# A mixture-of-experts stage on one core: the first token tile is turned and split in two halves, the second tile's transposes go inside the first product, and part of the next weights waits for the first gather

## What is computed

```
gate = jnp.sum(jax.nn.one_hot(ids, N_EXPERTS, dtype=jnp.float32) * wv[..., None], axis=1)
hid = jnp.einsum('td,edf->tef', t, w_up)
a, u = jnp.split(hid, 2, axis=-1)
act = jax.nn.silu(a) * u * gate.astype(hn.dtype)[..., None]
y = jnp.einsum('tef,efd->td', act, w_down)
```

## Time and profile before

| | |
|---|---|
| median of 3 runs | 883.4 us (883.09 to 884.41) |
| the profiled execution | 883.04 us |
| its span in the trace | 881.0 us, 2.04 us less than its time |
| PE busy, PEld, DVE, ACT, POOL | 90%, 71%, 68%, 40%, 35% of the span |
| the expert stage | from about 544 us to the end |

### The profile page before, as it was taken

How to read it: one execution, slowest core, us unless ns; L and a number is a source line. 1 busy time by engine, 2 the same in 40 slices (tenths; PEclk the granted TensorE clock), 3 DMA queues, 4 the chain that set the end, 5 groups by cost and what they waited for, 6 DMA issues and landing times. The chain is left out here.

```text
span 881.0 us, 13284 instructions
## 1 busy us (share of the span) xinstructions
PE 791.8 (90%) x4729; PEld 623.6 (71%) x4730; DVE 596.6 (68%) x701; ACT 354.3 (40%) x644; POOL 309.3 (35%) x248
## 2 busy tenths in 40 slices
PE   3899999999988899999999994199999999998593
PEld 3689999999945565667776883178888888887341
DVE  6779489742178965776786575994557997670097
ACT  3810111101345763454455343544444444443044
POOL 3000899940000101100000011155566888563046
PEclk9999999999968999999999995599999999999697
DMA  8956534530170501311102047867778997789664
GB/s 322 402 175 215 167 123 134 168 96 1 64 300 29 143 14 49 96 72 41 56 25 72 25 146 255 326 237 280 265 259 333 400 374 285 276 298 320 260 245 155
DMA packets 77361, 165.30 MB, mean 188 GB/s; under 512 B 7397, under 2 KB 32517, under 8 KB 75266
## 3 DMA queue, kind: packets, MB, share of 16 engines
q1 hardware_dynamic: 68402, 132.15, 42.7%
q0 software_dynamic: 7760, 28.31, 8.8%
q10 hardware_dynamic: 1152, 4.19, 1.3%
HBM read 132.57 MB, written 32.08 MB: 187 GB/s over the span
## 5 line engine op out<-in xcount | busy, mean ns | idle before, releaser
L2040 PE MATMUL psum<-we_hi,x_parts 128*128 x384 | 137.0, 403 | 0.8 <-ACT au L1897 0.8
L1703 DVE TENSOR_TENSOR we_lo<-we_raw,we_hi 128x2048 fp32r<-128x2048 f32 x48 | 116.5, 2433 | 1.4
L449 PE MATMUL psum<-hn_hi,w_hi 128*128 128x364 f32 (+1 forms) x384 | 91.3, 333 | 2.4 <-issue 2.4
L1701 DVE CAST we_hi<-we_raw 128x2048 fp32r<-128x2048 f32 x42 | 56.2, 1339 | 53.3 <-DMA we_raw<-in_w_up_dram 27.2
L449 PE MATMUL psum<-hn_lo,w_hi 128*128 128x364 f32 (+1 forms) x384 | 90.8, 332 | 0.0
L449 PE MATMUL psum<-hn_hi,w_lo 128*128 128x364 f32 (+1 forms) x384 | 90.5, 330 | 0.0
L1037 PE MATMUL psum<-wo_hi,mixin 128*128 128x512 f32 (+1 forms) x256 | 83.6, 398 | 0.0
L2040 PEld LDWEIGHTS psum<-we_hi,x_parts 128*128 128x128 f32 x384 | 72.3, 188 | 15.2 <-issue 1.0
L2040 PE MATMUL psum<-we_lo,x_parts 128*128 x192 | 75.3, 392 | 0.0
L630 DVE SCALAR_TENSOR_TENSOR proj<-wm,cT,proj 128x2048 f32<-128x2048 f32 x28 | 72.5, 2637 | 0.0
L449 PEld LDWEIGHTS psum<-hn_hi,w_hi 128*128 128x128 f32 x384 | 67.3, 190 | 6.3 <-issue 6.0
(11 more groups left out here) (315 smaller groups left out, 1584.6 us busy)
## 6 DMA issues: line engine op xcount, KB each, us to landing
we_raw<-in_w_up_dram SPq DMA_DIRECT2D x32, 1024.0 KB, 8.1
wm<-in_w_mod_dram SPq DMA_DIRECT2D x16, 1024.0 KB, 5.6
we_raw<-in_w_down_dram SPq DMA_DIRECT2D x16, 1024.0 KB, 6.1
w_raw<-in_w_in_dram SPq DMA_DIRECT2D x16, 512.0 KB, 6.3
we_raw<-ff_d SPq DMA_DIRECT2D x12, 512.0 KB, 6.4
proj<-in_x_prompt_dram SPq DMA_DIRECT2D x4, 1024.0 KB, 8.0
sc_room<-in_w_mod_dram SPq DMA_DIRECT2D x4, 1024.0 KB, 14.2
proj<-in_w_mod_dram SPq DMA_DIRECT2D x2, 2048.0 KB, 12.0
```

Of the source, the lines that this page charges most:

```text
L449: mm = pe.matmul(psum[:, 3 * slot + c, 0:n], w[:, slot, k, :], hn[:, k, t0:t0 + n], start=(k == 0 and w is w_hi and hn is hn_hi), stop=(k ...
L1701: dve.tensor_copy(we_hi[:, a:b], raw).then_inc(wh_ready, 1)
L1703: dve.tensor_tensor(we_lo[:, a:b], raw, we_hi[:, a:b].bitcast(F32), ALU.subtract).then_inc(ready, 1)
L2040: mm = pe.matmul(psum[:, 2, :], x[:, s, k, :], w[:, bass.ds(at + k * 2 * DE, 2 * DE)], start=(k == 0 and x is x_hi and w is we_hi), stop=( ...
```

## The change

Five things are changed together.

1. SP: within expert 1, the second half of `w_up` (and so also its `w_down`, and expert 2, which come behind it in SP's program) waits for `gathered[0]` 16, that is for the landing of the first gather. Expert 2 no longer waits for `x_turned`.
2. PE: tile 0 is turned and lowered in two halves of four transposes and one product (`turn_first`, `lower_first`), each half with its own semaphore count.
3. ACT: tile 0's high and low part are copied in two halves of 128 x 512 (`high_first`, `low_first`) in place of copies of 128 x 1024. `up` of tile 0 waits for the first half ahead of k = 0 and for the second half ahead of k = 4.
4. PE: tile 1's eight transposes stand no longer ahead of `up` of tile 0 but inside it, after k = 4, and its `lower_x` after k = 6 (before: after k = 2).
5. The counts that the others wait for are moved up by one, since tile 0 now counts twice. POOL's third gather waits, as before, for the whole turned tile 0.

```diff
--- before.py
+++ after.py
@@ -1548,6 +1548,8 @@
                     sp.wait_ge(down_ready, e - (NW - 1))
                     sp.wait_ge(up_done, last)
                 for half in range(2):
+                    if e == 1 and half == 1:
+                        sp.wait_ge(gathered[0], 16)
                     a, b = at + half * UP // 2, at + (half + 1) * UP // 2
                     sp.dma_start(we_raw[:, a:b].rearrange("p (k n) -> p k n", k=KC // 2),
                                  up[:, half * KC // 2:(half + 1) * KC // 2, :]).then_inc(up_loaded[s][half], 16)
@@ -1557,7 +1559,6 @@
 
             for e in range(FIRST):
                 load(e)
-            sp.wait_ge(x_turned, 1)
             for e in range(FIRST, NW):
                 load(e)
             sp.wait_ge(tables_ready, 1)
@@ -1813,10 +1814,10 @@
 
             fetch_first(0, None)
             fetch_first(1, None)
-            fetch_first(2, 1)
-            fetch_first(3, 2)
+            fetch_first(2, 2)
+            fetch_first(3, 3)
             gate_act(0, None)
-            fetch_first(4, 3)
+            fetch_first(4, 4)
             gate_act(1, 1)
             less = pool.value_load(ntile[0:1, 0:1], min_val=SLOT_TILES_MIN // 2 - 1, max_val=SLOT_TILES // 2 - 2)
             with pool.Fori(1, less + 1) as i:
@@ -1869,13 +1870,23 @@
                     act.wait_ge(loaded, 16)
                     act.activation(we_hi[:, a:b], we_raw[:, a:b], ACT.Copy).then_inc(first_hi, 1)
 
+            def high_first(half):
+                act.wait_ge(x_turned, 1 + half)
+                src = psum[:, half, :].rearrange("p (k c) -> p k c", c=P)
+                act.activation(x_hi[:, 0, 4 * half:4 * half + 4, :], src, ACT.Copy).then_inc(xh_copied, 1)
+
+            def low_first(half):
+                act.wait_ge(x_lowed, 1 + half)
+                src = psum[:, half, :].rearrange("p (k c) -> p k c", c=P)
+                act.activation(x_lo[:, 0, 4 * half:4 * half + 4, :], src, ACT.Copy).then_inc(x_ready, 1)
+
             def high_x(t, s):
-                act.wait_ge(x_turned, t + 1)
+                act.wait_ge(x_turned, t + 2)
                 src = psum[:, 0:2, :].rearrange("p b (k c) -> p (b k) c", c=P)
                 act.activation(x_hi[:, s, :, :], src, ACT.Copy).then_inc(xh_copied, 1)
 
             def low_x(t, s):
-                act.wait_ge(x_lowed, t + 1)
+                act.wait_ge(x_lowed, t + 2)
                 src = psum[:, 0:2, :].rearrange("p b (k c) -> p (b k) c", c=P)
                 act.activation(x_lo[:, s, :, :], src, ACT.Copy).then_inc(x_ready, 1)
 
@@ -1909,8 +1920,10 @@
 
                 act.activation(idst[:, s:s + 1], ids[:, bass.ds(t, 1)], ACT.Copy).then_inc(idst_ready, 1)
 
-            high_x(0, 0)
-            low_x(0, 0)
+            high_first(0)
+            high_first(1)
+            low_first(0)
+            low_first(1)
             high_x(1, 1)
             low_x(1, 1)
             swish(0, None)
@@ -2001,8 +2014,19 @@
                                    start=(k % 4 == 0), stop=(k % 4 == 3), is_transpose=True, skip_group_check=True)
                 mm.then_inc(x_turned, 1)
 
+            def turn_first(half):
+                for k in range(4 * half, 4 * half + 4):
+                    mm = pe.matmul(psum[:, half, (k % 4) * P:(k % 4 + 1) * P], xg[:, 0, k * P:(k + 1) * P], ident[:, :],
+                                   start=(k % 4 == 0), stop=(k % 4 == 3), is_transpose=True, skip_group_check=True)
+                mm.then_inc(x_turned, 1)
+
+            def lower_first(half):
+                pe.wait_ge(xh_copied, 1 + half)
+                pe.matmul(psum[:, half, :], minus[:, :], x_hi[:, 0, 4 * half:4 * half + 4, :].rearrange("p k c -> p (k c)"),
+                          start=False, stop=True, skip_group_check=True).then_inc(x_lowed, 1)
+
             def lower_x(t, s):
-                pe.wait_ge(xh_copied, t + 1)
+                pe.wait_ge(xh_copied, t + 2)
                 for half in range(2):
                     mm = pe.matmul(psum[:, half, :], minus[:, :], x_hi[:, s, 4 * half:4 * half + 4, :].rearrange("p k c -> p (k c)"),
                                    start=False, stop=True, skip_group_check=True)
@@ -2030,10 +2054,13 @@
 
             def up(t, s, place, copied, between):
                 e, at = place
-                pe.wait_ge(x_ready, t + 1)
+                if not (isinstance(t, int) and t == 0):
+                    pe.wait_ge(x_ready, t + 2)
                 if copied is not None:
                     pe.wait_ge(au_copied, copied)
                 for k in range(KC):
+                    if isinstance(t, int) and t == 0 and k % (KC // 2) == 0:
+                        pe.wait_ge(x_ready, 1 + k // (KC // 2))
                     if k % (KC // 2) == 0:
                         pe.wait_ge(up_ready, e * 2 + (1 + k // (KC // 2)))
                     for x, w in ((x_hi, we_hi), (x_hi, we_lo), (x_lo, we_hi)):
@@ -2057,7 +2084,9 @@
                 mm.then_inc(down_done, 1)
 
             def step0(k):
-                if k == 2:
+                if k == 4:
+                    turn_x(1, 1, 16, 2)
+                elif k == 6:
                     lower_x(1, 1)
 
             def step1(k):
@@ -2068,14 +2097,16 @@
                 elif k == 5:
                     lower_act(0)
 
-            turn_x(0, 0, 16, None)
-            lower_x(0, 0)
+            pe.wait_ge(gathered[0], 16)
+            turn_first(0)
+            turn_first(1)
+            lower_first(0)
+            lower_first(1)
             pe.wait_ge(oneh_ready, 2)
             by_slot(7, 2, 6)
-            turn_x(1, 1, 16, 1)
             first, second = places(1)
             up(0, 0, first, None, step0)
-            turn_x(2, 0, 32, 2)
+            turn_x(2, 0, 32, 3)
             up(1, 1, second, 1, step1)
             down(0, first, None)
             less = pe.value_load(ntile[0:1, 0:1], min_val=SLOT_TILES_MIN // 2 - 1, max_val=SLOT_TILES // 2 - 2)
@@ -2089,7 +2120,7 @@
                         lower_act(t - 1)
 
                 if gathers is not None:
-                    turn_x(t + 1, 1 - s, gathers, t + 1)
+                    turn_x(t + 1, 1 - s, gathers, t + 2)
                 before, this = places(t)
                 up(t, s, this, t, steps)
                 down(t - 1, before, t - 1)
@@ -2108,7 +2139,7 @@
             lower_act(less * 2 + 3)
             down(less * 2 + 3, places(less * 2 + 4)[0], less * 2 + 3)
             pe.wait_ge(rows2_in, 16)
-            pe.wait_ge(x_ready, less * 2 + 4)
+            pe.wait_ge(x_ready, less * 2 + 5)
             half_row(l2g_row, l2g, 0)
             half_row(l2g_row, l2g, 1).then_inc(tail_sums, 1)
```

## The result

| | before | after |
|---|---|---|
| median | 883.6 us (883.09 to 884.41) | 897.0 us (896.07 to 898.47, 4 runs) |
| profiled execution | 883.04 us | 896.44 us |
| PE busy | 791.8 us | 794.7 us |

The ratio is 1.0146, with a 95% interval of 1.0128 to 1.0165. The forecast was 891.4 us, with 894.5 as the upper end.

A forecast was written before the change was run, and what follows sets the result against it. PE bounds the kernel: its tile loop has no gap, so delay ahead counts in full. 5.3 + 0.9 + 1.6 + 0.2 = 8.0 us on 883.04 gives 891.0, plus 0.4 for the median: 891.4 us; range 888.5 to 894.5.

The forecast's parts named there:

- The gather: First gather, with later weights held back: takes 4.5 us, landing at 567.0 instead of 569.1, a gain of 2.1 us.
- The rival that it isn't faster: First gather's 6.56 us could be descriptor work on POOL; all 2.1 us later, 893.5 us; chance 0.10.
- The held transfers are those that ACT waits for: ACT's casts precede tile 0's copies in order; the last cast would end at 577.85, against 570.2 before.
- I take 8.4: landing at 575.9: Expert 1's `w_down`, issued near 567.5, takes 8.4 us to land; ends 574.2 and 576.6.
- no cost: Expert 2's loads land behind expert 1's, near 585, ahead of DVE's need, hidden behind PE's products.
- First product at +5.3: After ACT's release, copies, lowering and gate products: the first product starts at 582.0 against 576.68, +5.3 us.
- Inside the first product: Tile 1's eight transposes move into the first product, 0.88 us at full clock: +0.9 us.
- Between the first and the second product: ACT's table load loses its cover behind tile 1's low copy; PE issues at +3.4 instead of 1.8: +1.6 us.
- The rival of a drain: A drain behind ACT's table load, exposed between the first two products: 892.5 us; chance 0.02.
- The clock: PE's clock rises at 582.2, just after the first product has begun: +0.2 us, ends 0 and 1.5.
- the clock stays low longer: Whole first product at half speed, as PE's work comes in pieces with a long pause: about 897 us; chance 0.04.
- The tile loop has no gap: PE is busy for 190.00 of 190.00 us between 594 and 784 us, so any delay ahead moves all that follows.

The follow-up runs named there:

- experiment 7: Changed kernel, with expert 2's transfers and POOL's third gather issued only when expert 1's `w_down` has landed: 894.6 us, one run.
- experiment 9: Changed kernel, with expert 2's transfers and the second and third gathers issued only when expert 1's `w_down` has landed: 896.0 us, one run.
- experiment 5: Changed kernel with the hold kept, the two casts that wait for held transfers moved from ACT to DVE: 883.6 us, ratio 0.9986 to the original.
- experiment 4: Changed kernel plus a one-column sigmoid on ACT behind tile 0's low copies, making the table load early: 894.8 us, ratio 1.0122 to the original.
- experiment 1: Original kernel with only SP's wait moved (the hold alone), tile 0 turned whole, transposes as before: 893.2 us, ratio 1.0098.
- experiment 2: Changed kernel without the hold, SP's original order restored, halves and moved transposes kept: 884.5 us, ratio 1.0008 to the original.
- experiment 3: Changed kernel, with expert 2's three transfers issued only when expert 1's `w_down` has landed: 895.5 us, ratio 1.0136 to the original.

## Why the prediction was right in kind and short in size

- **The gather**: landing forecast 567.0, measured 567.02. The rival that it isn't faster is wrong (4.47 us against 6.56). The Trainium skill (DMA: Bandwidth & Descriptors, "Queues, rings and completion order") says that a DMA engine takes turns between the rows that have work. Experiments 7 and 9 agree in kind, in the other direction: gathers on POOL's queue slow the weights on SP's, by 1.0 and 2.2 us. In size the prediction's estimate from it, 1.3 us lost, falls short of the 2.1 that holding gave.
- **"The held transfers are those that ACT waits for"**: right, and shown by experiment 5.
- **"I take 8.4: landing at 575.9"**: this step failed. It measured 11.70, landing at 579.2, 3.3 us of the 5.4 by which the sum was short. The nearest row, 9.1 us, was of a pair beside the third gather, and the third gather (its "gather 2") is all the company that the prediction gave to `w_down`. The pair with that gather is 7.5 + 1.0 us by experiments 7 and 9, just the 8.4 forecast. What it left out measured the rest: 2.2 us for the tail of the second gather, which is still in flight when the held transfers start, and 1.0 for expert 2's transfers, which SP now issues right behind. Those it had put at "no cost", looking only at who waits for them and not at what they delay.
- **First product at +5.3**: the rest of that path measured as forecast, from the cast's end at 581.08 to the product at 585.13, 4.1 us against 4.15.
- **"Inside the first product" +0.9**: 0.88 for the eight transposes and some 0.5 us of low clock, against 0.2 in the clock's term.
- **"Between the first and the second product" +1.6**: measured 1.6. The table load lost its cover, and experiment 4 shows it. The rival of a drain is wrong. The Trainium skill (ScalarE: Activation LUTs, "What ACT_TABLE_LOAD costs") gives 1.28 us and a drain of 1.38 behind it. The load took 1.28, but the sigmoid started 0.02 us later.
- **"The clock" +0.2**: this step failed too, by 1.9 us. I looked for the clock only where PE starts up, and not where the new gap of 3.5 us lets it fall. The second product measured 1.6 us longer, the first 0.5. The two failed terms together, 3.3 and 1.9, are 5.2 of the 5.4 us. The rival "the clock stays low longer" named the right time, 897, by luck: it had the whole first product at half speed, 6 us, where 1 us of it ran so, and the rest of the 897 is the landing.
- **The tile loop has no gap**: right, 190.00 of 190.00.
- **Small slips in the sums**, none of which changes the outcome: 582.1 + 0.5 + 6.7 is 589.3 and not 589.5; 894.2 with half a us is 894.7 and not 894.5; and the low end is 888.5 in one place and 888.0 in another.

By parts timed alone: hold +8.7, halves -1.8, transposes and table load +2.5, together 9.4 of the 12.9 us that the ratio gives. The other 3.5 us are no more than the intervals leave open, since the hold's alone reaches 3 us either way. Counted within the traces, from the start of the stage to tile 3's transposes, hardly anything is left over: 49.2 us before, 62.3 after, 59.2 in experiment 1 and 52.2 in experiment 2. So the hold alone adds 10.0 us and the rest of the change 3.0, together 13.0 of 13.1. Each is one trace, and the clock takes its part in each of them: it falls in the changed kernel's gap (1.6 us), and it rises late in experiment 2.

Two things stay open. The clock fell in the gap of about 3.5 us, or within half a us behind it, in all four traces that have the long pause of ACT's wait ahead and nothing added in the gap (after, experiments 3, 7, 9: pauses of 12.5, 11.5, 10.5 and 8.3 us). It didn't in experiments 2 and 5, which have the same gap but no pause between tile 0's turning and its lowering. What decides isn't shown. And the second gather's tail costs `w_down` 2.2 us, while all of its 0.5 MB are 1.3 us at 414 GB/s; why was not tried.

## What to carry to other kernels

Before a transfer is held back, look up which engine's program waits for it, and what stands behind that wait. Here it was right to hold the transfer (2.5 us gained, with its casts moved), and wrong to leave its cast on ACT, ahead of the copies that set the pace. A wait also has a price where it ends: count what goes out in the same microsecond, and look at every gap that it makes in PE's work for the clock, since the same work behind it may run slower; work that must be done anyway and has no hurry (the gate products) is what such a gap is for.

## What was not expected of the hardware

- PE's clock fell from 1.00 to 0.53 at 596.5, after a gap of 3.5 us with 1.06 us of transposes in it, and stayed low to about 599.9. With twelve small products (1.53 us) added in the gap it stayed up.
- The rise varies as well. PE's work is the same up to the first product in experiments 2 and 5, and its lowering starts at 571.6 in both traces. In the one the clock rises at 579.1. In the other it is up already inside the gate products, which take 1.63 us instead of 2.50. Such a difference is 2 us or so of one trace's time, and one trace per kernel doesn't show how often it comes.
- 1 MB behind another MB by itself landed in 7.5 us, and in 9.7, 10.7 and 11.7 as a gather, a second one and expert 2's 3 MB came beside it (one trace each; with all of them the traces vary from 10.9 to 11.8).
